# A hybrid decoder step on one core: the compression's first layer in three fp32r passes over pairs of batches, and the gate slots of attention ahead of u's

## The reference

```python
def compress(rows, params):
    w1, b1, w2, b2 = params
    n_cmp = (T - 32) // 16 + 1
    idx = jnp.arange(n_cmp)[:, None] * 16 + jnp.arange(32)[None, :]
    blocks = rows[:, idx].transpose(0, 1, 3, 2, 4).reshape(B, n_cmp, G, 32 * dh)
    return jax.nn.gelu(blocks @ w1 + b1) @ w2 + b2
```

## Time and profile before

| | |
|---|---|
| median of 3 runs | 626.97 us (624.81 to 627.13) |
| the profiled execution | 627.12 us, of which 625.4 are its span from the first to the last instruction |
| mean granted TensorE clock | 0.991 of full speed |
| busy: TensorE, VectorE, ScalarE, GpSimd | 589.9, 310.3, 230.6, 76.5 us |
| compression stage | 132 us, from 100 to 232 us |

### The profile page before, as it was taken

The page is one execution under the profiler, slowest core; times in us unless marked ns, Lnnn a source line. Parts: engine busy times, 40 slices in busy tenths (PEclk is TensorE's granted clock), DMA queues, the critical chain, the costliest instruction groups (busy, mean ns, idle before and its releaser), DMA issues.

```text
span 625.4 us, 12374 instructions
## 1 busy us (share of the span) xinstructions
PE 589.9 (94%) x5118; PEld 515.0 (82%) x5118; DVE 310.3 (50%) x785; ACT 230.6 (37%) x529; POOL 76.5 (12%) x127
## 2 busy tenths in 40 slices
PE   7899998999899999998999999999999999998993
PEld 5899997887888887997898887666567899997992
DVE  5722224051675223463474656767654447762265
ACT  5543345140323113332332544445353342222333
POOL 0017432020201115404200000000000000000000
PEclk9999998999999999999999999999999999998998
DMA  9347722643612316933722120201111433306104
GB/s 301 140 122 234 263 70 81 254 124 103 204 63 82 105 35 201 309 96 110 262 69 69 48 60 30 68 2 34 35 35 35 124 89 89 114 2 237 35 2 143
DMA packets 45673, 69.99 MB, mean 112 GB/s; under 512 B 4145, under 2 KB 36081, under 8 KB 45362
## 3 DMA queue, kind: packets, MB, share of 16 engines
q1 hardware_dynamic: 38016, 44.84, 23.1%
q0 software_dynamic: 6880, 23.24, 11.2%
q10 hardware_dynamic: 722, 1.12, 0.5%
HBM read 65.22 MB, written 8.13 MB: 117 GB/s over the span
## 4 chain that ended last, share of the span: by engine, by line
PE 88%; DVE 6%; ACT 3%; DMA 2%; issue 1%; ACTq 0%; SPq 0%; DVEq 0%
PE m L1530 53%; PE s L1697 10%; PE s L1821 4%; PE o L1835 4%; PE t L1828 3%; PE t L1672 2%; PE t L1723 2%; DMA U<-in_x_p 2%; PE m L1611 2%; DVE U L1274 1%; PE s L1737 1%; PE o L1782 1%; PE t L1661 1%; ACT U L903 1%; PE o L1808 1%
## 5 line engine op out<-in xcount | busy, mean ns | idle before, releaser
L1530 PE MATMUL m<-h_hi,w_hi 128*128 128x272 f32 x448 | 133.1, 297 | 0.0
L1530 PE MATMUL m<-h_hi,w_lo 128*128 128x272 f32 x448 | 129.2, 288 | 0.0
L1530 PE MATMUL m<-h_lo,w_hi 128*128 128x272 f32 x448 | 128.7, 287 | 0.0
L1530 PE MATMUL m<-w_hi,h_hi 128*128 128x256 f32 (+2 forms) x360 | 104.9, 291 | 3.6 <-DVE U L1478 2.0
L1530 PE MATMUL m<-w_lo,h_hi 128*128 128x256 f32 (+2 forms) x360 | 102.5, 285 | 0.0
L1530 PE MATMUL m<-w_hi,h_lo 128*128 128x256 f32 (+2 forms) x360 | 102.4, 284 | 0.0
L1530 PEld LDWEIGHTS m<-h_hi,w_hi 128*128 128x128 f32 x448 | 84.2, 188 | 10.0 <-issue 7.3
L1164 DVE TENSOR_TENSOR w_lo<-raw,w_hi 128x1024 fp32r<-128x1024 f32 (+2 forms) x62 | 71.2, 1156 | 37.4 <-ACT w_hi L916 37.3
L1530 PEld LDWEIGHTS m<-h_hi,w_lo 128*128 128x128 f32 x448 | 84.5, 189 | 0.0
L1530 PEld LDWEIGHTS m<-h_lo,w_hi 128*128 128x128 f32 x448 | 84.5, 189 | 0.0
L1530 PEld LDWEIGHTS m<-w_hi,h_hi 128*128 128x128 f32 (+1 forms) x360 | 68.4, 190 | 5.5 <-DVE U L1478 2.3
(11 more groups left out here) (278 smaller groups left out, 885.8 us busy)
## 6 DMA issues: line engine op xcount, KB each, us to landing
raw<-in_w_in SPq DMA_DIRECT2D x36, 512.0 KB, 4.0
U<-in_x_p SPq DMA_DIRECT2D x8, 512.0 KB, 7.1
raw<-in_w_o SPq DMA_DIRECT2D x8, 512.0 KB, 4.1
raw<-in_w_in SPq DMA_DIRECT2D x8, 256.0 KB, 3.8
U<-in_ck_win POOLq DMA_DIRECT2D x8, 256.0 KB, 3.4
U<-in_cv_win POOLq DMA_DIRECT2D x8, 256.0 KB, 5.9
raw<-in_w_pa SPq DMA_DIRECT2D x8, 256.0 KB, 4.1
raw<-in_w_pb SPq DMA_DIRECT2D x4, 512.0 KB, 3.4
```

The source lines that it names most:

```text
L1530: ins = mm(out, lhs(a, k), rhs(b, k), start=(k == 0 and a + b == 0), stop=(k == n - 1 and a == 1))
```

## The change

- Each half of the compression now has the prompt's chunk first (`c % 5 == 0`), then four chunks of two batches (`PAIRS`), ten chunks in all (`NCH`).
- A pair's hidden layer is done in three fp32r passes. ScalarE splits `w1` into `w1_hi` (step `w1hi`), VectorE makes `w1_lo` (step `w1lo`). Every transposed tile is cast to `xt_hi` by ScalarE and subtracted to `xt_lo` by VectorE. Step `hidh` has the two passes with `xt_hi` (32 products), `hidl`, behind the next pair's first two tiles, the pass with `xt_lo` (16). Both heads and both batches stand in one product of 4 x 63 = 252 columns, interleaved: in `xt_hi` neighbouring blocks of one head and batch are four words apart.
- The 252 columns of a product are contiguous for each of the 32 row offsets, as the cache rows are gathered by parity (`CMP_ROW`, `cmp_rows`): even rows of eight tokens on partitions 0 to 63, odd ones on 64 to 127. The prompt's rows are loaded in two transfers.
- The prompt chunks stay plain fp32 and use space in `sg`.
- One main group per chunk and one after the last (`IN_CHUNK`); `ln2` behind chunks 6 and 7, `sp` behind 8 and 9.
- The slots ZA0 and ZA1 come before U0 and U1, with the counts of semaphores made from the list (`z_count`, `mix_count`).
- At the start, the sample rows' sum of squares (`("sq", NT)`) moves ahead of `("hT", 1)`, and the third slot's `split` and `low` move one group earlier. An unused warm-up (`WARM = 0`) is removed.

```diff
+         ("ZA0", "tr", C_ZA, 256), ("ZA1", "tr", C_ZA, 256),
          ("U0", "tr", C_U, 256), ("U1", "tr", C_U + 256, 256),
-         ("ZA0", "tr", C_ZA, 256), ("ZA1", "tr", C_ZA, 256),
...
+CMP_ROW = 2 * (np.arange(P) % 64) + np.arange(P) // 64
...
+NCH = 10
+PAIRS = [c for c in range(NCH) if c % 5]
+IN_CHUNK, AFTER_LAST_HIDDEN = (1, 1, 1, 1, 1, 1, 1, 1, 1, 1), 1
...
-    order += [("hT", 1), ("low", 1, 0), ("split", 1, 1), ("low", 1, 1), ("sq", NT), ("sq", 2), ("sq", 3), ("ms", 2, NT)]
+    order += [("sq", NT), ("hT", 1), ("low", 1, 0), ("split", 1, 1), ("sq", 2), ("low", 1, 1), ("sq", 3), ("ms", 2, NT)]
...
+    order += [("w1hi", 0)]
+    for c in range(NCH):
+        behind = [("hidl", c - 1)] if c - 1 in PAIRS else []
+        if c % 5 == 0:
+            order += [("xt", c, 0)] + behind
+            main(IN_CHUNK[c])
+            if c:
+                order += [("w1hi", 1), ("w1lo", 1), ("kc", c - 1)]
+            order += [("hid", c)]
+            if c == 0:
+                order += [("w1lo", 0)]
+            continue
+        order += [("xt", c, 0), ("xt", c, 1)] + behind
+        main(IN_CHUNK[c])
+        order += [("xt", c, 2), ("xt", c, 3), ("kc", c - 1), ("hidh", c)]
+        order += {6: [("ln2", i) for i in range(3)], 7: [("ln2", i) for i in range(3, NT + 1)],
+                  8: [("sp", i) for i in range(3)], 9: [("sp", i) for i in range(3, NT + 1)]}.get(c, [])
+    order += [("hidl", NCH - 1)]
+    main(AFTER_LAST_HIDDEN)
+    order += [("kc", NCH - 1)]
...
+        def turned(x, r, g, b):
+
+            return x[64 * r:64 * r + 64, :].rearrange("p (q o n g b) -> p q o n g b", q=4, o=2, g=G, b=2)[:, :, :, :, g, b]
...
                 if b == "p":
-                    src = pk_cmp if w == "kc" else pv_cmp
-                    pool.dma_start(ring[0:64, n % RING, :], src.rearrange("(m r) c -> m (r c)", r=8)).then_inc(done, 16)
+                    pool.wait_ge(cmp_out, 32)
+                    src = (pk_cmp if w == "kc" else pv_cmp).rearrange("(m o r) c -> o m (r c)", o=2, r=8)
+                    for o in range(2):
+                        pool.dma_start(slot[32 * o:32 * o + 32, :], src[o, :, :]).then_inc(done, 16)
...
+                elif kind == "w1hi":
+                    act.wait_ge(w1_loaded[s[1]], 16)
+                    if s[1]:
+                        act.wait_ge(hid_sum, 5)
+                    else:
+                        act.wait_ge(t_done, T_AT[("qTs",)] + 1)
+                        act.wait_ge(out_done, 16 * (N_OUT - 1))
+                        act.wait_ge(cmp_out, 32)
+                    for k in range(2):
+                        ins = nc.scalar.copy(w1_hi[k][:, :, :], w1_at[s[1]][:, 8 * k:8 * k + 8, :])
+                    ins.then_inc(w1_hi_done, 1)
+                elif kind == "xt" and s[1] in PAIRS:
+                    c, n = s[1], s[2]
+                    b, r = divmod(n, 2)
+                    act.wait_ge(t_done, t + 1)
+                    if c > 1:
+                        act.wait_ge(hid_half, PAIRS.index(c))
+                    for g in range(G):
+                        ins = nc.scalar.copy(turned(xt_hi, r, g, b), TB[t % 2][64 * g:64 * g + 64, :].rearrange("p (q o n) -> p q o n", q=4, o=2))
+                    ins.then_inc(xt_hi_done, 1)
...
+                elif kind == "w1lo":
+                    dve.wait_ge(w1_hi_done, s[1] + 1)
+                    dve.wait_ge(hid_sum, 5 if s[1] else 1)
+                    for k in range(2):
+                        ins = v.tensor_tensor(w1_lo[:, 8 * k:8 * k + 8, :], w1_at[s[1]][:, 8 * k:8 * k + 8, :], w1_hi[k][:, :, :].bitcast(F32), ALU.subtract)
+                    ins.then_inc(w1_lo_done, 1)
...
+                    dve.wait_ge(xt_hi_done, 4 * PAIRS.index(c) + n + 1)
+                    for g in range(G):
+                        ins = v.tensor_tensor(turned(xt_lo, r, g, b), tb[64 * g:64 * g + 64, :].rearrange("p (q o n) -> p q o n", q=4, o=2),
+                                              turned(xt_hi, r, g, b).bitcast(F32), ALU.subtract)
                     ins.then_inc(t_dve, 1)
...
+                elif kind in ("hidh", "hidl"):
+                    c = s[1]
+                    out = S[c % 2]
+                    first = kind == "hidh"
+                    if first:
+                        pe.wait_ge(w1_hi_done, c // 5 + 1)
+                        pe.wait_ge(w1_lo_done, c // 5 + 1)
+                        pe.wait_ge(xt_hi_done, 4 * PAIRS.index(c) + 4)
+                        if c >= 2:
+                            pe.wait_ge(hid_ready, c - 1)
+                    else:
+                        for n in range(4):
+                            wait_evacuated(pe, T_AT[("xt", c, n)])
+                    for j in range(16):
+                        o, q = divmod(j, 4)
+                        at = 512 * q + 256 * (o % 2) + 4 * (o // 2)
+                        end = at + 4 * NCS
+                        w = w1_hi[j // 8][:, j % 8, :]
+                        if first:
+                            mm(out[:, 0:end - at], w, xt_hi[:, at:end], start=(j == 0), stop=False, skip_group_check=True)
+                            ins = mm(out[:, 0:end - at], w1_lo[:, j, :], xt_hi[:, at:end], start=False, stop=False, skip_group_check=True)
+                        else:
+                            ins = mm(out[:, 0:end - at], w, xt_lo[:, at:end], start=False, stop=(j == 15), skip_group_check=True)
+                    ins.then_inc(hid_half if first else hid_sum, 1)
```

More of the change, by code:

```diff
@@ L223, in plan @@
     order += [("hT", 3)]
-    main(4)
+    main(3)
     order += [("split", 2, 0)]
     main(1)
-    order += [("low", 2, 0), ("split", 2, 1)]
-    main(1)
-    order += [("low", 2, 1)]
+    order += [("low", 2, 0), ("split", 2, 1), ("low", 2, 1)]
+    main(2)
     order += [("out_cmp",), ("wsT",), ("rope", 0)]
@@ L387 @@
 RING = 3
-LOADS = [(w, b) for w in ("kc", "vc") for b in list(range(NB)) + ["p"]]
+LOADS = [(w, b) for w in ("kc", "vc") for b in ["p"] + list(range(NB))]
 LOAD_AT = {x: n for n, x in enumerate(LOADS)}
@@ L397, with load_of, ring_count @@
 NPT = 4
-def part(c):
-    return ("kc" if c < 3 else "vc"), c % 3
+def load_of(c, n):
+    return LOAD_AT[("kc" if c < 5 else "vc", "p" if c % 5 == 0 else 2 * (c % 5 - 1) + n // 2)]
 def load_turned(n):
     w, b = LOADS[n]
-    c = (0 if w == "kc" else 3) + (2 if b == "p" else b // QB)
-    return T_AT[("xt", c, 0 if b == "p" else 2 * (b % QB) + 1)] + 1
+    c = 0 if w == "kc" else 5
+    return T_AT[("xt", c, 0) if b == "p" else ("xt", c + 1 + b // 2, 2 * (b % 2) + 1)] + 1
+def ring_count(n):
+    return sum(32 if LOADS[k][1] == "p" else 16 for k in range(n % RING, n + 1, RING))
 def key_freed(n):
@@ L425, in slot_used, with z_count, mix_count @@
     return max(n for n, x in enumerate(MAIN) if x[1] == sl) + 1
-def hid_count(c):
-    return [0, 2, 4, 5, 7, 9, 10][c]
-FN_AT = {x: n for n, x in enumerate(x for x in MAIN if SLOTS[x[1]][0][0] in "UZ")}
+FN = [x for x in MAIN if SLOTS[x[1]][0][0] in "UZ"]
+FN_AT = {x: n for n, x in enumerate(FN)}
+def z_count(k):
+    return sum(1 for x in FN[:k + 1] if SLOTS[x[1]][0][0] == "Z")
+def mix_count(k):
+    return sum(1 for x in FN[:k + 1] if not SLOTS[x[1]][0].startswith("ZA"))
 ROPE_STEPS = [12, 24, 36, 48]
@@ L843, in _ @@
                     store(pv_cmp, sv_cmp, kq[:, 0:NT, 384:512], kq[0:TS, NT, 384:512], cmp_out)
-                    pool.wait_ge(rows_ready, 3)
-                    load_upto(RING)
+                    pool.wait_ge(rows_ready, 4)
+                    for n in range(1, RING):
+                        load(n)
                 elif s[0] == "rope":
@@ L851, in _ @@
                         if s[1] == 0:
+                            load(0)
+                            loaded[0] = RING
                             store(pk_sel, sk_sel, kq[:, 0:NT, c0:c0 + 128], kq[0:TS, NT, c0:c0 + 128], out_done)
@@ L1538, in _ @@
                     wait_t_bank(pe, t)
-                if kind == "warm":
-                    pe.wait_ge(pads_zero, 1)
-                    zeros = q_bd[:, 0:4, :].rearrange("p b n -> p (b n)")
-                    for _ in range(WARM):
-                        mm(O[:, 0:P], zeros, zeros, start=True, stop=True)
+                if kind == "spread":
                     pe.wait_ge(st_ready, 2)
@@ L1708, in _ @@
                             for k, w2 in enumerate(("w2k", "w2kr")):
-                                ins = mm(S[2][64 * g:64 * g + 64, 256 * k:256 * k + n], pm(w2), x, start=True, stop=True)
-                    elif c < 5:
-                        for b in range(QB):
+                                ins = mm(S[2][64 * g:64 * g + 64, 256 * k:256 * k + n].rearrange("p (b n) -> p b n", n=step)[:, :, 0:nn], pm(w2), src, start=True, stop=True)
+                    else:
+                        for b in range(n // step):
@@ L1712, in _ @@
                             for g in range(G):
[L1713 to L1717 removed]
+                                a = g * n + b * step
@@ L1718, in _ @@
```

(1 more changed line is left out.)

212 lines of the change are left out of this document (90 added, 122 removed).

## The result

The changed kernel takes 663.1 us by the median of its runs (661.4 to 665.7), the kernel before 627.1 beside it (624.8 to 628.8): a ratio of 1.058, 95% interval 1.0532 to 1.0629. The forecast of 626.3 us and its range up to 640 both missed it. The profiled execution took 665.7 us, with a span of 663.8.

A forecast was written before the change was run, and what follows sets the result against it. TensorE, busy 94% of the span, was taken as the bound. Stage -3.2 us, table loads +2.7 and the rest -0.4 summed to -0.9, from 627.1 to 626.3 us; own range 623 to 631, with rivals 617 to 640.

The forecast's parts named there:

- The products: Compression stage: four fp32 hidden chunks (58.0 us) become 384 fp32r products of 252 columns (45.3 us), a gain of 12.7 us.
- narrow fp32r: Rival, chance 0.04: below 256 columns fp32r products run as slowly as fp32, giving 755 us.
- second layer: Compression's second-layer products: key groups become four of half the width, costing 1.7 us more; values unchanged.
- The evacuation of a transposed tile: Compression stage: ScalarE casts, VectorE subtracts, at 0.58 and 0.69 us a copy; both engines' work still fits beside TensorE's.
- The rival of strided writes: Rival, chance 0.13: high and low parts written four words apart slow the copies; +13.6 us, so 640 us.
- the forecast's case: The main forecast, chance 0.50: 626.3 us, its own range 623 to 631.
- The new wait: Before each pair's high products TensorE waits for ScalarE's high parts: 12.5 us over eight pairs, bounds 4 and 17.
- The old waits: Compression stage: today's waits on VectorE's transpose evacuation (8.3 us) and issue (1.6) disappear in their old form, 9.9 us.
- The starts of the halves: Waits at the start of keys and of values, plus the last pair's spatial products: 5.2 us, bounds 2 and 9.
- The table loads: ScalarE, Gelu and Exp alternating behind the reordered gate slots: four more loads, +2.7 us; rival in full, chance 0.10, 630 to 632.
- The rest: Gathers, prompt load and small moves cost nothing; the third slot's earlier split may save 0.4 us.

The follow-up runs named there:

- the last kernel: Changed kernel with copies two words apart, u's Gelus between the exponentials, next weights' rounding behind the high products, and unused filler products: 627.2 us, ratio 0.9993.
- The square: Four medians: changed kernel 663.1 us, with unused filler products 652.9, with copies two words apart 637.2, with both 635.7.
- the fillers: Extra products no result uses, issued ahead of TensorE's waits; 20 ahead of each pair's high products in the changed kernel: 652.9 us, ratio 1.0436.
- the kernel at two words: Changed kernel with a pair's two batches innermost, so copies write every second word instead of every fourth: 637.2 us, ratio 1.0172.

## Why the prediction was wrong, step by step

**The products** were right in kind: at full clock 252 columns take 115 to 121 ns in the high products and 121 to 125 in the low ones, and narrow fp32r did not come. TensorE's saving, products less second layer, was put at 12.7 - 1.7 = 11.0 us and came to 14.4 in the last kernel by busy times, or some 12.7 without the half clock that the kernel before met.

**The evacuation of a transposed tile** is the step that failed: "the cast costs what a copy does: 588 ns". That row is a contiguous write; the new write is four words apart and took 1066 ns, and VectorE's 1076 where 687 was put. The rival of strided writes had named the mechanism, its place and the point from which it decides (0.68 us), and was given 0.13. The evidence against it was weak: the earlier trace rows is a read of PSUM, and what failed here is access to SBUF. A row of one memory was taken as excluding a cost of the other.

**The rival's own price**, 640 us, was too low by 23 us. It counted ScalarE alone, 13.6 us. The square gives 17.2 for the strides with the clock held, VectorE's included, and 10.2 more for the clock, which no term of the sum had. The remaining 8.6 us, in a kernel whose clock held through the whole stage, are of the kinds that the forecast's case had, new waits and table loads, and what the fillers cost.

**The new wait** was sized at 12.5 us with copies at their old price. With copies near that price it measured 16.1: the mechanism was right, the size 3.6 us short. With the weight roundings out of the way it was 13.4, where the prediction had 1.0 us a pair for the keys and 1.0 to 1.5 for the values, some 9.5: the wait without a rounding is 1.7 to 1.8 us in seven of eight pairs, and this is the mis-sized part. The 0.2 us to refill stood in no row; in the runs the first product starts 0.15 to 0.26 us behind the end of the last copy.

**The old waits** were put at 9.9 us from the chain's shares. By the earlier trace rows TensorE is idle for only 132.0 - 124.6 = 7.4 us of the stage, so some 2 us of the gain were never there. The end of the sum has a slip too, of no weight: 627.1 - 0.9 is 626.2.

**The starts of the halves** were put at 5.2 us, 2.8 of them for the value side, and were not what failed. In the kernel at two words TensorE waits 2.4 us for VectorE's subtractions at the start of the value side, 1.2 for the first prompt chunk's rows and 0.3 at the spatial products. The square root and the norms do stand in line, as the prediction said, but TensorE has work of its own meanwhile, and the runs that moved them found little to gain.

**The table loads** were right in number, four more, and near in price: 2.7 us forecast, 3.2 more in the stretch, 2.6 of them gone with two loads. **The rest** held: the transposes of the queries ahead of the stage started 0.9 us earlier (95.98 against 96.86), where 0.4 was forecast, and nothing changed behind the key transposes.

## What to carry to other kernels

Before a tile is laid out anew, look at the byte step of each write and each read of it in SBUF, on every engine; here 8 bytes cost next to nothing and 16 bytes 0.4 to 0.5 us a copy, and putting the pair innermost, an edit of a few lines, cured it. On a TensorE that is the bound, price a new wait with what the clock may lose behind it: in the changed kernel eight waits of 1.8 to 3.1 us cost some 10 us more than their length, and work without use in them paid for itself; in the kernel at two words it gave 1.5 us. And when a faster product shortens only one engine's part, add up the chain per step (tile, copy, copy, product), since busy time left room here on both helpers and yet each step waited.

## What the runs showed of the hardware that was not expected

A 64x512 fp32 copy from PSUM to SBUF as fp32r took ScalarE 579 (contiguous), 614 (every second word) and 1066 ns (every fourth), and VectorE's subtraction 687, 689 and 1076. VectorE pays it once for any operand: 1064 ns with only a read at four words, 1083 with only the write, 1076 with both. TensorE reading 252 moving columns as pairs 16 bytes apart took 227 to 231 ns at granted clocks from 0.60 to 0.78 and 229 at 1.00, against about 120 for runs. The granted clock fell to 1.2 GHz behind idle stretches of 1.8 to 3.1 us in all eight pairs of the changed kernel, and of 1.7 to 1.8 us in some pairs of other kernels and not in others; behind three of 2.6 us in the kernel at two words it held, and behind one of 1.2 us it fell. What decides is not shown. Such a kernel scatters: 631.3 to 638.7 us in four runs with the weight roundings late, where the kernel at two words with its waits filled stayed within 634.5 to 636.9.
